# A sparse-expert router and a final norm at the seams of a 4-millisecond kernel: logits from the residual, and the last norm in two groups

## The reference, cut to what matters

```python
x = x + mod[:, 2] * x_out
h2 = _rmsnorm(x, norm2_w[i]) * (1.0 + mod[:, 4]) + mod[:, 3]
x = x + mod[:, 5] * _expert_choice_ffn(h2, w_router[i], w_exp_gate[i], w_exp_up[i], w_exp_down[i])
...
return _rmsnorm(x, final_norm_w)
...
def _rmsnorm(x, w):
    xf = x.astype(F32)
    y = xf * lax.rsqrt(jnp.mean(xf * xf, axis=-1, keepdims=True) + EPS)
...
def _expert_choice_ffn(h, w_router, w_gate, w_up, w_down):
    aff = jax.nn.softmax((h @ w_router).astype(F32), axis=-1)
    gate, idx = lax.top_k(jnp.swapaxes(aff, 1, 2), cap)
    xe = h[bidx, idx]
    a = jnp.einsum('becd,edf->becf', xe, w_gate)
    u = jnp.einsum('becd,edf->becf', xe, w_up)
    ye = jnp.einsum('becf,efd->becd', jax.nn.silu(a) * u, w_down) * gate[..., None]
```

## Time and profile before

| | |
|---|---|
| median of 3 runs | 4092.66 us (4091.35 to 4096.43) |
| the profiled execution: time, span | 4090.83 us, 4089.0 us |
| TensorE busy over the span | 3670.1 us (90%) |
| from the last projection's end to the first expert matmul | about 3161.5 to 3261.4 us |
| the experts | about 3261 to 4041 us |
| from the last scatter to the end | 4041.3 to 4089.0 us |

### The profile page before, as it was taken

One profiled execution on the slowest core, in us unless ns is written; L12 is line 12 of the kernel. 1 busy time (PEld: TensorE's weight loads), 2 busy tenths in 40 slices (PEclk: granted clock), 3 DMA queues, 4 the chain that ended last, 5 costly groups with the idle time before them and its releaser, 6 DMA issues.

```text
span 4089.0 us, 45856 instructions
## 1 busy us (share of the span) xinstructions
PE 3670.1 (90%) x18363; PEld 2942.8 (72%) x18363; DVE 2193.9 (54%) x2890; ACT 1551.9 (38%) x1929; POOL 707.6 (17%) x325
## 2 busy tenths in 40 slices
PE   7988887998989989999999879999659599999995
PEld 5555555666868767888887647777547599999995
DVE  3333333535325655454433452636553699999985
ACT  3333332223322222122222342333342467777675
POOL 2000001101212322222222211111002012222210
PEclk9999999999999999999999989999889699999997
DMA  3111111213345313444421113121512499999995
GB/s 117 37 36 42 47 36 67 84 57 124 125 160 189 131 45 133 157 145 136 136 68 60 33 56 145 70 103 68 180 54 114 199 358 376 380 383 378 383 369 202
DMA packets 126100, 611.64 MB, mean 150 GB/s; under 512 B 14217, under 2 KB 15633, under 8 KB 101058
## 3 DMA queue, kind: packets, MB, share of 16 engines
q1 hardware_dynamic: 121138, 591.41, 39.1%
q0 software_dynamic: 4608, 16.78, 1.6%
q10 hardware_dynamic: 144, 0.52, 0.0%
HBM read 525.35 MB, written 83.27 MB: 149 GB/s over the span
## 4 chain that ended last, share of the span: by engine, by line
PE 62%; DVE 7%; ACT 3%; DMA 2%; issue 2%; POOL 0%; SPq 0%; ACTq 0%; DVEq 0%; POOLq 0%
PE bank L263 13%; PE bank L265 13%; PE bank L264 13%; PE bank L2918 4%; PE bank L2917 4%; PE bank L2916 4%; PE bank L2928 2%; PE bank L2926 2%; PE bank L2927 2%; DVE stg L1511 1%; PE bank L2699 1%; DMA D_acc<-aq,iT 1%; PE bank L280 0%; DVE EL L2849 0%; PE bank L1126 0%
## 5 line engine op out<-in xcount | busy, mean ns | idle before, releaser
L263 PE MATMUL bank<-XH,WH 128*128 128x512 f32 (+1 forms) x2696 | 1103.8, 409 | 116.9 <-DVE XL L1910 15.8
L264 PE MATMUL bank<-XL,WH 128*128 128x512 f32 (+1 forms) x2696 | 1060.5, 393 | 0.0
L265 PE MATMUL bank<-XH,WL 128*128 128x512 f32 (+1 forms) x2696 | 1059.7, 393 | 0.0
L251 POOL TENSOR_TENSOR WL<-WR,WH 128x1024 fp32r<-128x1024 f32 (+1 forms) x249 | 489.6, 1966 | 2387.2 <-ACT WH L243 2387.2
L263 PEld LDWEIGHTS bank<-XH,WH 128*128 128x128 f32 x2696 | 512.9, 190 | 301.0 <-issue 80.9
L264 PEld LDWEIGHTS bank<-XL,WH 128*128 128x128 f32 x2696 | 514.2, 191 | 118.2 <-issue 9.0
L265 PEld LDWEIGHTS bank<-XH,WL 128*128 128x128 f32 x2696 | 512.8, 190 | 118.5
L243 ACT ACTIVATE WH<-WR 128x1024 fp32r<-128x1024 f32 (+1 forms) x249 | 216.5, 870 | 644.2 <-PE bank L265 624.2
L2849 DVE TENSOR_TENSOR EL<-ER,EH 128x2816 fp32r<-128x2816 f32 x120 | 369.2, 3082 | 1.7 <-ACT EH L2844 1.7
L2844 ACT ACTIVATE EH<-ER 128x2816 fp32r<-128x2816 f32 x120 | 306.4, 2562 | 149.1 <-PE bank L2918 87.4
L2916 PE MATMUL bank<-EH,WH 128*128 128x352 f32 x1024 | 335.4, 328 | 6.3 <-DVE EL L2849 6.3
(11 more groups left out here) (476 smaller groups left out, 5160.6 us busy)
## 6 DMA issues: line engine op xcount, KB each, us to landing
ER<-in_wu_dram SPq DMA_DIRECT2D x48, 1408.0 KB, 9.4
ER<-in_wd_dram SPq DMA_DIRECT2D x40, 1408.0 KB, 10.1
aq<-in_w_ada_dram SPq DMA_DIRECT2D x96, 512.0 KB, 3.8
WR<-in_w_in_dram SPq DMA_DIRECT2D x89, 512.0 KB, 4.4
ER<-in_wg_dram SPq DMA_DIRECT2D x32, 1408.0 KB, 8.7
res<-in_wg_dram SPq DMA_DIRECT2D x16, 1408.0 KB, 8.4
res<-in_wu_dram SPq DMA_DIRECT2D x16, 1408.0 KB, 8.4
WR<-in_wg_dram SPq DMA_DIRECT2D x16, 1408.0 KB, 8.8
```

The lines of the kernel that those rows point to most:

```text
L251: e.tensor_tensor(WL[:, n % 2 * 1024:n % 2 * 1024 + m], raw, hi.bitcast(F32), ALU.subtract).then_inc(*w_lo.up("w_lo", n))
L263: e.matmul(bank[bk][:, 0:b - a], whi, xhi, start=k == 0, stop=False)
L264: e.matmul(bank[bk][:, 0:b - a], whi, xlo, start=False, stop=False)
L265: mm = e.matmul(bank[bk][:, 0:b - a], wlo, xhi, start=False, stop=k == K - 1)
```

## The change

In `out2`:

- The router's weights are scaled by `cs_` (s) into `wrs`, 32 columns a chunk of which 16 hold zeros, ahead of the first output tile; the bias part `b W` is summed into `wrc` and made by one matmul of ones.
- The logits are made with the scaled weights as the weights and the residual itself as the moving side: 16 matmuls of 512 columns into banks 2 and 3, chunk j writing the 32 output partitions that begin at 32 (j mod 4). A 17th row, from two more matmuls with `w9`, is the sum of squares.
- Both banks are copied to `lg4`, and 8 matmuls with `rsel` (17 columns) turn each 128 tokens to rows and add the four groups. Ln and Exp of the 17th column give r (`rs8`, 8 columns), and VectorE multiplies, adds the bias, and goes on with the softmax as before.
- `rstd_pe` and `rstd_act` come after that. `h2` is now made by 8 products on GpSimd (`res` times `acq`) and by ScalarE with scale and bias.
- The rows of `res` (for `D_acc`) are turned and stored first, then those of `h2`, with three row buffers and four banks in place of two and eight. Pieces 2 and 3 are issued between the two sets, once `res` is free, and the small load of the router's weights moves ahead of the first weight tiles.

In the final norm all 8 chunks are loaded at once, the roots are taken for chunks 0 to 3 and 4 to 7 together, the squares of chunks 4 and 5 are made by VectorE, and the result is written in place.

The diff, cut to its core:

```diff
-    orw, wr_ = WR[:, 0:2 * T], WR[:, 2 * T:2 * T + 128]
+    orw = [WR[:, i * T:(i + 1) * T] for i in range(3)]
+    wr_, wrs, wrb, w9 = (ac2[:, a:b] for a, b in ((128, 256), (256, 512), (512, 640), (640, 672)))
+    rsel, wrc, cr_, rs8 = (ac2[:, a:b] for a, b in ((672, 689), (704, 720), (720, 736), (736, 744)))
+    lg4 = WR[:, 0:T]
...
-        for s, dram in enumerate((D_h, D_acc)):
+        for s, dram in enumerate((D_acc, D_h)):
+            if s:
+                e.wait_ge(*on("out2.turn", 0, 7, 1))
+                e.wait_ge(*on("out2.x", 7))
+                e_load(e, 2)
+                e_load(e, 3)
             for tc in range(8):
                 e.wait_ge(*on("out2.row", s, tc, 1))
+                n = 8 * s + tc
+                e.dma_start(dram[tc * 128:tc * 128 + 128, :], orw[n % 3]).then_inc(*d_row[n % 3].up("out2.stored", n))
+        for n in range(13, 16):
+            e.wait_ge(*on("out2.stored", n))
         e_load(e, 4)
...
+        e.wait_ge(*on("out2.wrs"))
+        e.wait_ge(*on.bank(1, "out2.c"))
+        e.matmul(bank[1][:, 0:16], ones, wrc, start=True, stop=True).then_inc(*P.up("out2.cp"))
+        for h in range(2):
+            e.wait_ge(*on.bank(2 + h, "out2.lg4", h))
+        for j in range(8):
+            for h in range(2):
+                r4_ = slice(j % 4 * 32, j % 4 * 32 + 32)
+                e.wait_ge(*on("out2.res", j, h))
+                e.matmul(bank[2 + h][r4_, :], wrs[:, j * 32:j * 32 + 32], xc(j)[:, half(h)], start=j < 4,
+                         stop=j > 4)
         e.wait_ge(*on("out2.sum"))
+        for h in range(2):
+            e.matmul(bank[2 + h][0:32, :], w9, acq[:, half(h)], start=False, stop=True).then_inc(*P.up("out2.lgp", h))
+
+        e.wait_ge(*on.bank(0, "out2.soft"))
+        for tc in range(8):
+            o = tc % 4 * 64 + tc // 4 * 32
+            e.wait_ge(*on("out2.lg4", tc // 4))
+            mm = e.matmul(bank[0][:, o:o + 17], lg4[:, tc * 128:tc * 128 + 128], rsel, start=True, stop=True)
+        mm.then_inc(*P.up("out2.route"))
         rstd_pe(e, acq, T, (6, 7), ("out2",))
-        e.wait_ge(*on("out2.wr"))
-        e.wait_ge(*on.bank(2, "out2.soft"))
-        for j in range(8):
-            e.wait_ge(*on("out2.h", j))
-            for tc in range(8):
-                o = tc % 4 * 32 + tc // 4 * 16
-                mm = e.matmul(bank[2][:, o:o + 16], tj(h2, j)[:, tc * 128:tc * 128 + 128], wr_[:, j * 16:j * 16 + 16],
-                              start=j + tc == 0, stop=j + tc == 14)
-        mm.then_inc(*P.up("out2.route"))
-        for s, src in enumerate((h2, res)):
+        for s, src in enumerate((res, h2)):
             for tc in range(8):
                 for q in range(2):
-                    b = (2 * tc + q) % 8
+                    b = 4 + (2 * tc + q) % 4
+                    if s:
+                        e.wait_ge(*on("out2.h", 4 * q + 3))
                     e.wait_ge(*on.bank(b, "out2.row", s, tc, q))
...
-        rstd_act(e, acq, 1024, T, (6, 7), ("out2",))
+        e.wait_ge(*on("w_lo", NT - 1))
+        e.wait_ge(*on("out2.lgp", 0))
+        e.activation(lg4[:, 0:512], bank[2][:, :], AF.Copy).then_inc(*A.up("out2.lg4", 0))
+        l3 = bank[0][:, 0:256].rearrange("p (c x) -> p c x", x=32)
+        e.wait_ge(*on("out2.route"))
+        e.activation(rs8.unsqueeze(2), l3[:, :, 16:17], AF.Ln, scale=1.0 / 1024, bias=cn("eps")).then_inc(*A.up())
+        e.wait_ge(*A.now)
+        e.activation(rs8, rs8, AF.Exp, scale=-0.5).then_inc(*A.up("out2.r8"))
         e.wait_ge(*on("out2.sub"))
         e.activation(af, af, AF.Exp).then_inc(*A.up("out2.exp"))
-        e.wait_ge(*on("w_lo", NT - 1))
+        rstd_act(e, acq, 1024, T, (6, 7), ("out2",))
+            if s:
+                for j in range(8):
+                    e.wait_ge(*on("out2.x", j))
+                    e.activation(tj(h2, j), tj(h2, j), AF.Identity, bias=mod[:, 24 + j, 0:1],
+                                 scale=cs_[:, 16 + j:17 + j]).then_inc(*A.up("out2.h", j))
+                    if n >= 3:
+                        e.wait_ge(*on("out2.stored", n - 3))
+                    e.activation(orw[n % 3][:, half(q)], bank[4 + (2 * tc + q) % 4][:, :], AF.Copy).then_inc(
                         *A.up("out2.row", s, tc, q))
...
+        w3 = wr_.rearrange("p (j e) -> p j e", e=16)
+        e.memset(w9[:, 16:17], 1.0).then_inc(*V.up())
+        e.tensor_tensor(wrs.rearrange("p (j e) -> p j e", e=32)[:, :, 0:16], w3, b3(cs_[:, 16:24], 16), ALU.mult).then_inc(
+            *V.up())
+        e.tensor_tensor(wrb.rearrange("p (j e) -> p j e", e=16), w3, b3(mod[:, 24:32, 0], 16), ALU.mult).then_inc(*V.up())
+        e.wait_ge(*V.now)
+        e.tensor_reduce(wrc, wrb.rearrange("p (j e) -> p e j", e=16), AX.X, ALU.add).then_inc(*V.up("out2.wrs"))
...
-        e.wait_ge(*on("out2.lo", 1, 7))
-        for j in range(8):
-            e.wait_ge(*on("out2", "rstd", 1))
-            e.scalar_tensor_tensor(tj(h2, j), xc(j), cs_[:, 16 + j:17 + j], acq, ALU.mult, ALU.mult).then_inc(
-                *V.up("out2.x", j))
+        e.wait_ge(*on("out2.lgp", 1))
+        e.tensor_copy(lg4[:, 512:1024], bank[3][:, :]).then_inc(*V.up("out2.lg4", 1))
+        e.wait_ge(*on("out2.cp"))
+        e.tensor_copy(cr_, bank[1][:, 0:16]).then_inc(*V.up("out2.c"))
+        l3 = bank[0][:, 0:256].rearrange("p (c x) -> p c x", x=32)[:, :, 0:16]
         a3 = af.rearrange("p (c e) -> p c e", e=16)
+        e.wait_ge(*on("out2.r8"))
+        e.tensor_tensor(a3, l3, b3(rs8, 16), ALU.mult).then_inc(*V.up("out2.soft"))
+        e.wait_ge(*V.now)
+        e.tensor_tensor(a3, a3, cr_.unsqueeze(1).broadcast_to([128, 8, 16]), ALU.add).then_inc(*V.up())
+        e.wait_ge(*V.now)
+        e.tensor_reduce(mx, a3, AX.X, ALU.max).then_inc(*V.up())
+        e.wait_ge(*V.now)
+        e.tensor_tensor(a3, a3, b3(mx, 16), ALU.subtract).then_inc(*V.up("out2.sub"))
         e.wait_ge(*on("out2.exp"))
...
+        e.wait_ge(*on("out2.lo", 1, 6))
+        e.wait_ge(*on("out2", "rstd", 1))
+        for j in range(8):
+            e.tensor_tensor(tj(h2, j), xc(j), acq, ALU.mult).then_inc(*o2_pool.up("out2.x", j))
...
+    fx, fss = [ER[tc // 2][:, tc % 2 * 1024:tc % 2 * 1024 + 1024] for tc in range(8)], hN[:, 0:8]
...
-            i = tc % 4
-            if tc >= 4:
-                e.wait_ge(*on("f.y", tc - 4))
-            e.dma_start(ER[i][:, 0:1024], D_acc[tc * 128:tc * 128 + 128, :]).then_inc(*d_fl[i].up("f.in", tc))
-            if tc >= 3:
+            e.dma_start(fx[tc], D_acc[tc * 128:tc * 128 + 128, :]).then_inc(*d_fl[tc].up("f.in", tc))
+        for tc in range(8):
+            e.wait_ge(*on("f.y", tc))
+            e.dma_start(out[tc * 128:tc * 128 + 128, :], fx[tc]).then_inc(*d_fs[tc % 4].up("f.out", tc))
...
+        for g in range(2):
+            for tc in ((0, 1, 2, 3), (6, 7))[g]:
+                e.wait_ge(*on("f.in", tc))
+                if tc in (2, 3, 6, 7):
+                    e.wait_ge(*on("f.sq", tc - 2 if tc < 4 else tc - 4))
+                e.activation(yout[tc % 2], fx[tc], AF.Square, accum_out=fss[:, tc:tc + 1]).then_inc(*A.up("f.sq", tc))
+            s4 = fss[:, 4 * g:4 * g + 4]
             e.wait_ge(*A.now)
-            e.activation(ss, ss, AF.Ln, scale=1.0 / 1024, bias=cn("eps")).then_inc(*A.up())
+            if g:
+                e.wait_ge(*on("f.sq", 5))
+            e.activation(s4, s4, AF.Ln, scale=1.0 / 1024, bias=cn("eps")).then_inc(*A.up())
             e.wait_ge(*A.now)
-            e.activation(ss, ss, AF.Exp, scale=-0.5).then_inc(*A.up("f.rstd", tc))
+            e.activation(s4, s4, AF.Exp, scale=-0.5).then_inc(*A.up("f.rstd", g))
...
+        for tc in (4, 5):
+            e.wait_ge(*on("f.in", tc))
+            e.tensor_tensor_reduce(yout[tc % 2 + 2], fx[tc], fx[tc], 1.0, 0.0, ALU.mult, ALU.add,
+                                   fss[:, tc:tc + 1]).then_inc(*V.up("f.sq", tc))
+        e.wait_ge(*on("fnw"))
         for tc in range(8):
-            i = tc % 4
-            xr, yo, ss = ER[i][:, 0:1024], yout[i], hN[:, i * 4:i * 4 + 1]
-            e.wait_ge(*on("f.rstd", tc))
-            e.wait_ge(*on("fnw"))
-            e.scalar_tensor_tensor(yo, xr, ss, fnw, ALU.mult, ALU.mult).then_inc(*V.up("f.y", tc))
```

More of the change, by code:

```diff
@@ L2626, in program @@
     d_xb2, d_wr, d_m5 = dma_sem("out2_xb"), dma_sem("out2_wr"), dma_sem("out2_m5")
-    d_row = [dma_sem(f"out2_row{i}") for i in range(2)]
+    d_row = [dma_sem(f"out2_row{i}") for i in range(2)] + [d_m5]
     NR, NH, PW = 8, 5, 2816
@@ L2658, in out2_sp @@
             e.dma_start(xc(j), D_xb[j]).then_inc(*d_xb2.up("out2.xb"))
+        e.dma_start(wr_, I["w_router"]).then_inc(*d_wr.up("out2.wr"))
         e.wait_ge(*on("out2.m5"))
@@ L2834, in program @@
     d_acc, d_mf, d_fnw = dma_sem("acc"), dma_sem("mf"), dma_sem("fnw")
-    d_fl, d_fs = d_yin, [dma_sem(f"fs{i}") for i in range(4)]
+    d_fl, d_fs = d_yin + d_gate + d_xin[0:1], [dma_sem(f"fs{i}") for i in range(4)]
```

(16 more changed lines are left out.)

38 lines of the change are left out of this document (9 added, 29 removed).

## The result

The changed kernel takes 4054.76 us (median of 4 runs, 4052.18 to 4057.95) against 4094.55 us (4 runs, 4091.35 to 4098.46) of the kernel before on the same chip: a ratio of 0.9903, 95% interval 0.9886 to 0.9920. 4055 was forecast. The gain is 39.8 us by these medians, where 38.3 was forecast. The profiled execution took 4057.95 us with a span of 4056.1.

What follows compares the result with a forecast made beforehand. TensorE fills the expert loop (777.39 of 780 us), left alone; the gain is where it waits or crawls, router and final norm. 22.3 + 16.0 = 38.3 off 4090.8 gives 4052.5, with 1.8 for the median said as 4055; range 4047 to 4070.

Steps and rivals of the forecast that it cites:

- Router to top-k: From the projection's last take-over to the top-k: top-k starts at 3176.5 instead of 3202.8 and ends 26.2 us earlier.
- Two table loads, Ln, Exp on 8 columns: In the router, ScalarE's roots before the softmax: 1.28 + 0.29 + 1.28 + 0.2 and hops, 3.2 us.
- Ten small instructions at nothing: VectorE's work on router weights ahead of the projection's first tile: about 2.5 us, hidden by idle time, so no cost.
- GpSimd doesn't hold the top-k: In the router, VectorE's one-input top-k is not held by GpSimd's products; rival that it is: 4070 us, 8%.
- the slow and the held products of the rivals: GpSimd's eight h2 products: slow, 10.8 us more, 4065 us, 8%; held until the top-k is done, 4089 us, 3%.
- The stores as what is late next: At the join behind the router: h2 stores, all done about 3217.4, outlast the top-k; join 22.3 us earlier.
- 2.9 MB and 4.2 MB at 412 GB/s are 17.2 us, and one hop of 1.5 in front: Before the join: pieces 2 and 3, then h2 rows, issued from 3198.6, all stored at about 3217.4.
- Without the two pieces in front it would be 3213.3, the top-k's end: At the join: if pieces 2 and 3 don't delay the h2 rows, it goes with the top-k; 4050.5 us.
- the rival of a lost rhythm: In the expert loop: TensorE waits for each of 192 pieces; gain gone at 0.2 us each, 4112 at 0.3; 2%.
- Final norm: Last product ends at 4069.8 instead of 4085.9, 16.0 us earlier; 15.4 of the 16 from 12 fewer table loads.
- The rival in which they don't run at once: Router logits matmuls on column groups take 13.7 us instead of 3.4: 4065 us; no or half grouping together 9%.
- If a group's matmul can only start when the one ahead in the queue has started: Router logits rival of in-order starts: 10.7 us instead of 3.4, time 4062; no or half grouping together 9%.

Runs made afterwards that it cites:

- e4_rows_first: The changed kernel with expert pieces 2 and 3 loaded behind the rows of h2 instead of ahead of them: 4049.49 us, ratio 0.9892.
- e6_roots_each: The changed kernel with the final norm's Ln and Exp taken chunk by chunk, sixteen table loads instead of four: 4070.73 us, ratio 0.9939.

## Why the prediction was right, point by point

By the traces the gain is 39.3 us where 38.3 was forecast: 22.3 at the join, 0.6 from there to the first expert matmul, 0.3 in the loop, 16.4 to the last product, and 0.3 given back behind it. That the median came out within 0.3 us of 4055 is luck: the kernel before stood 1.9 us higher in the new runs (4094.55 against 4092.66), which nearly balances the 1.5 by which the gain (39.8 by the medians) was larger. The sum itself ends at 4054.3 (4052.5 and 1.8), not 4054.5.

**Router to top-k: right, 1.5 us too careful.** MAX8 was forecast 15.0 us behind the take-over and came at 13.54, so the top-k ends 27.7 us earlier, not 26.2. The logits took 3.68 (3.4 forecast), the second copy, turning matmuls and products what I gave them. The step that was off is "Two table loads, Ln, Exp on 8 columns" with its 3.2 us: the table load at 3173.14 ran while its activation still waited for the turning matmuls (Ln starts at 3175.24, 0.82 after the load), so one of the two loads cost nothing. I had put it behind the wait. The rows of before don't show this case: their load at L288 belongs to a warm-up that waits for nothing.

**Ten small instructions at nothing: right.** In the projection TensorE idles 7.1 us ahead of L263, 7.2 before.

**GpSimd doesn't hold the top-k: right, with a gap.** 0.66 to 0.68 an instruction beside L2863, also with twice as many products; but the closing copies are held when a product is there. The rule that I told names the two-port mode too; I applied it to the top-k's instructions alone and not to the copies behind them. The products took 2.35 (2.41 forecast); the slow and the held products of the rivals did not occur.

**The stores as what is late next: right in the result (22.3 us earlier, forecast 22.3), by two errors that cancel.** That part is luck. The last product ended 34.7 us behind the take-over (3202.59), 2.3 earlier than the 37.0 of the sum, from the table load above and the hops I rounded up. Then from the issue of the pieces to the join it took 21.4 us, not 18.8. The term that was mis-sized is "2.9 MB and 4.2 MB at 412 GB/s are 17.2 us, and one hop of 1.5 in front": 7.1 MB in 21.4 us is 332 GB/s. The sum took the rows as ready whenever the DMA engines were. They are not: ScalarE's steps on `h2` did not follow each product, as I had it, but came eight in a row from 3195.60, behind the rows of `res`, and ended 2.2 us behind the last product (3204.76) instead of 1.2. The first store of `h2` was issued 3.9 us after the pieces, and with three buffers the fourth row's copy waited 4.29 us for that store to land behind the pieces. "Without the two pieces in front it would be 3213.3, the top-k's end" was wrong by 1.8 us (e4_rows_first): there 17.6 us pass from the last product to the join, where a hop of 1.5 and 4.2 MB at 412 GB/s would be 11.7. So the pieces were priced too high (7.0 for 3.9) and the rows too low, by 5.9. How the steps, TensorE's turning at half clock and the three buffers share that, no run here separates.

**Behind the join: unchanged, right.** 20.84 us instead of 21.45 to the first expert matmul. The loop kept its length in every kernel, also with its pieces 2 and 3 issued 14 us later: the rival of a lost rhythm fell.

**Final norm: right.** 16.4 us to the last product in the two full profiles (16.0 forecast), 16.1 over all with the final norm alone. Its reason, "12 of 16 table loads are gone, 15.4 us of the 16", was told too simply: with early transfers the twelve table loads are worth 14.3, but without early transfers grouping gives only 6.7 of the 16.4. The page "ScalarE: Activation LUTs" of the Trainium skill (What ACT_TABLE_LOAD costs) would add a drain of 1380 ns to each load; for these twelve that is an estimate of 31.9 us, and e6_roots_each shows 14.3, less than the loads alone. In this kernel the drain is not there.

**The column groups: right, and near an edge.** The rival in which they don't run at once was worth 10.3 by my sum and 10.3 at MAX8 when run. What I did not see is that the order of the matmuls matters: with eight records of a group in a row 4.2 of these 10.3 us are lost again. "If a group's matmul can only start when the one ahead in the queue has started" was the wrong question; what counts is how many of one group stand together.

## What to carry to other kernels

Where an edit takes time off a chain, work out what is late next with its own queue: here 5.4 of the 27.7 us went to stores that stood behind two large loads of the next stage, and moving those two loads gave 3.9 back at the join, of which 3.2 were left at the first expert matmul, with no loss in the loop. Grouping work on one engine (roots of four chunks) also groups what its results release, so it needs the inputs to be there already; test the two halves apart before giving either the credit. Small matmuls on different column groups should be queued so that few of one group stand together: four records in a row lost nothing here, eight in a row lost 4.2 us.
